# Output products of two mixers started earlier, with their high parts made by ScalarE

## The reference

```python
h = x
for i in range(2):
    u = rmsnorm(h, ln_mix[i])
    if i == 0:      # hs: 4 heads of 256 features; out = sigmoid(o) * rmsnorm(hs)
        mix = mlstm_mixer(u, mlstm_w_in, mlstm_b_gate, mlstm_norm, mlstm_w_out)
    else:           # o: 8 heads of 128 features; (rmsnorm(o) * (1 - lam_init)) @ w_out
        mix = diff_attention_mixer(u, diff_w_in, diff_lam, diff_norm, diff_w_out, i)
    h = h + mix
    h = h + square(relu(rmsnorm(h, ln_mlp[i]) @ w_up[i])) @ w_down[i]
return rmsnorm(h, ln_f)
```

## Time and profile before

| what | us |
|---|---|
| median of 3 runs | 2381.99 |
| lowest and highest of them | 2379.33, 2382.75 |
| the profiled execution: its own time | 2383.44 |
| its span in the trace | 2381.7 |
| TensorE busy in it (share of the span) | 2279.4 (96%) |
| VectorE, ScalarE, GpSimd busy | 1594.4, 888.8, 882.0 |

### The profile page before, as it was taken

One profiled execution on the slowest core, in us unless ns is written; L12 is line 12 of the kernel. 1 busy time (PEld: TensorE's weight loads), 2 busy tenths in 40 slices (PEclk: granted clock), 3 DMA queues, 4 the chain that ended last, 5 costly groups with the idle time before them and its releaser, 6 DMA issues.

```text
span 2381.7 us, 28693 instructions
## 1 busy us (share of the span) xinstructions
PE 2279.4 (96%) x10601; PEld 1880.6 (79%) x10601; DVE 1594.4 (67%) x1988; ACT 888.8 (37%) x1471; POOL 882.0 (37%) x672
## 2 busy tenths in 40 slices
PE   6999998899999999999899999987999999999998
PEld 5788886687888888888688888865878888888887
DVE  7534343569948749579467677775579849578396
ACT  3131122135434334344144444453145334343345
POOL 5433327410213233232476666656500233233230
PEclk9999999999999999999899999997999999999999
DMA  6111111246162442630522322212255352532601
GB/s 180 45 33 39 35 35 53 71 155 263 59 257 106 158 178 71 229 107 1 159 62 55 80 61 62 62 46 87 94 189 195 138 198 71 216 137 103 251 1 71
DMA packets 128834, 262.62 MB, mean 110 GB/s; under 512 B 7217, under 2 KB 81122, under 8 KB 121314
## 3 DMA queue, kind: packets, MB, share of 16 engines
q1 hardware_dynamic: 128290, 260.13, 32.2%
q10 hardware_dynamic: 448, 1.18, 0.1%
HBM read 202.56 MB, written 41.94 MB: 103 GB/s over the span
## 4 chain that ended last, share of the span: by engine, by line
PE 82%; DVE 8%; POOL 5%; ACT 2%; issue 2%; DMA 1%; SPq 0%; ACTq 0%; POOLq 0%; DVEq 0%
PE aps L913 10%; PE aps L915 9%; PE aps L917 9%; PE dps L813 6%; PE dps L815 6%; PE dps L814 5%; PE mps L913 3%; PE dps L913 3%; PE mps L915 3%; PE dps L915 3%; PE mps L917 3%; PE dps L917 3%; PE dps L795 3%; PE dps L796 3%; PE dps L797 3%; PE mps L1133 2%
## 5 line engine op out<-in xcount | busy, mean ns | idle before, releaser
L659 POOL TENSOR_TENSOR w_hi<-w_raw,ones 128x256 fp32r<-128x256 f32 (+1 forms) x127 | 175.7, 1404 | 486.9 <-PE dps L815 266.7
L813 PE MATMUL dps<-one_hi,w_hi 128*128 128x512 f32 x608 | 256.2, 421 | 1.2 <-POOL w_lo L664 1.2
L913 PE MATMUL aps<-b_ring,w_hi 128*128 128x512 f32 x640 | 249.9, 390 | 2.0 <-issue 2.0
L917 PE MATMUL aps<-b_ring,w_hi 128*128 128x512 f32 x640 | 249.0, 389 | 0.0
L915 PE MATMUL aps<-b_ring,w_lo 128*128 128x512 f32 x640 | 249.0, 389 | 0.0
L815 PE MATMUL dps<-one_lo,w_hi 128*128 128x512 f32 x608 | 238.5, 392 | 0.0
L814 PE MATMUL dps<-one_hi,w_lo 128*128 128x512 f32 x608 | 237.8, 391 | 0.0
L1708 DVE TENSOR_TENSOR b_ring<-h,b_ring 128x1024 fp32r<-128x1024 f32 x120 | 206.5, 1728 | 5.6 <-ACT b_ring L1322 5.6
L751 POOL TENSOR_TENSOR s_blk<-s_blk,a 128x1024 f32<-128x1024 f32 x24 | 68.6, 2860 | 377.6 <-DVE w_lo L1690 251.8
L664 POOL TENSOR_TENSOR w_lo<-w_raw,w_hi 128x256 fp32r<-128x256 f32 (+1 forms) x127 | 172.0, 1375 | 5.0
L795 PE MATMUL dps<-one_hi,w_hi 128*128 128x512 f32 x384 | 153.5, 400 | 11.8 <-POOL w_lo L664 4.9
(11 more groups left out here) (298 smaller groups left out, 5593.6 us busy)
## 6 DMA issues: line engine op xcount, KB each, us to landing
b_ring<-xs SPq DMA_DIRECT2D x42, 2048.0 KB, 7.9
xs<-b_ring SPq DMA_DIRECT2D x14, 2048.0 KB, 7.4
a<-in_w_up SPq DMA_DIRECT2D x16, 1024.0 KB, 5.4
a<-in_w_down SPq DMA_DIRECT2D x16, 1024.0 KB, 7.5
w_raw<-in_mlstm_w_in SPq DMA_DIRECT2D x24, 512.0 KB, 3.9
w_raw<-in_diff_w_in SPq DMA_DIRECT2D x24, 512.0 KB, 4.1
hspill<-h SPq DMA_DIRECT2D x2, 4096.0 KB, 12.8
h<-hspill SPq DMA_DIRECT2D x16, 512.0 KB, 3.4
```

The lines of the kernel that those rows point to most:

```text
L659: last = nc.gpsimd.tensor_tensor(w_hi[:, slot, cut], w_raw[:, slot, cut], ones[:, :].unsqueeze(1).broadcast_to([P, piece, P]), ALU.mult)
L813: nc.tensor.matmul(dps[:, half], w_hi[:, slot, k], rh, start=(k == 0), stop=False)
L913: nc.tensor.matmul(to[:, n], wh, ring[:, 0, k], start=new and k == 0, stop=False, skip_group_check=not new)
L917: last = nc.tensor.matmul(to[:, n], wh, ring[:, 1, k], start=False, stop=(k == 3), skip_group_check=not new)
```

## The change

The panels n = 0 and n = 1 of the output product both get their early tiles during the last head, and the work for that moves between engines:

1. Table `FILL` replaces `EARLY_AT`. It names for each place (step, part) the pairs (n, k) of panel and tile whose six products stand there. New places are (0, 1), ahead of the wait for `nm_ready` in layer 0, and (9, 0) and (9, 1), ahead of and behind the last transposes.
2. The early tiles' high parts are made by ScalarE (`high_early`, one instruction a tile): in layer 0 all six behind the sigmoid and ahead of the first step, in layer 1 behind the steps that `HIGH_AT` names. GpSimd makes only the low parts. ScalarE also makes the high parts of the weights of panels 1 and 2 (`high_out`), GpSimd their low parts (`split_out`). Panel 2 has its split weights in `a0_hi` and `a0_lo`, so that they needn't wait for a slot.
3. Panel 0's sum over the early tiles is added to `h` during the last head by VectorE (`add_partial`, in step 3 of layer 0 and step 6 of layer 1), which frees `dps` for panel 1. Its late tiles are summed in `mps` after the head and added by `add_rest`. Panel 1's late tiles follow in `dps`.
4. SyncE loads the weights of panels 2 and 3 ahead of the read-backs of `h`. The loop over the last panels is written out.

```diff
-    EARLY_AT = [[3, 4, 5, 6, 7, 8], [3, 4, 5, 6, 7, 8, 8]]
+    FILL = [{(0, 1): [(0, 0), (0, 1)], (1, 0): [(0, 2)], (1, 1): [(0, 3)], (2, 0): [(0, 4)], (2, 1): [(0, 5)],
...
+    PARTIAL_AT = [3, 6]
+
+    HIGH_AT = {2: [0, 1], 3: [2, 3], 4: [4, 5], 5: [6]}
...
         @block.gpsimd
...
-            def split_early(layer):
+            def split_early(layer, start, end):
 
                 hi, lo = one
-                pool.wait_ge(half_done, 2 * G_OUT[layer])
...
+                for t in range(start, end):
                     pool.wait_ge(y_early_hi, EARLY[0] * layer + t + 1)
...
+                            last = nc.gpsimd.tensor_tensor(
+                                lo[t // 4][:, half, t % 4, cut], h[:, t, half * HALF + c:half * HALF + c + PIECE * P],
+                                hi[t // 4][:, half, t % 4, cut].bitcast(f32), ALU.subtract)
                     last.then_inc(y_early, 1)
...
                 split(g, 1, (g + 1) // 2)
-                split_early(layer)
-                split(g + 1, 0, (g + 1) // 2)
-                pairs(g + 2, g + 8)
...
+                split_early(layer, 0, 4)
+                split_out(layer, 1)
+                split_early(layer, 4, EARLY[layer])
+                if layer == 0:
+                    pool.wait_ge(hy_ready, 2 * MH)
+                else:
+                    pool.wait_ge(on_ready, AH)
+                split_out(layer, 2)
+                for n in range(3, NT):
+                    split(g + n, (g + n) % 2, (g + n + 1) // 2)
...
         @block.tensor
...
+            def early_tile(layer, s, part):
+
+                g = G_OUT[layer]
+                for n, k in FILL[layer].get((s, part), []):
+                    last_k = EARLY[layer] - 1 if n == 0 else NT - 1
+                    if k == 0:
+                        pe.wait_ge(w_split, g + n)
                     pe.wait_ge(y_early, EARLY[0] * layer + k + 1)
-                    out_tile(layer, half, k)
+                    for half in range(2):
+                        if k == 0:
+                            pe.wait_ge(evac, 2 * (g + n) + half - 1)
+                        last = out_tile(layer, n, half, k, dps[:, half], 0, last_k)
...
+                for n in range(2):
+                    for half in range(2):
+                        for k in range(first, NT):
+
+                            pe.wait_ge(hid_ready, HID_OUT[layer] + LATE[layer] * half + k - first + 1)
+                            if n == 0:
+                                last = out_tile(layer, 0, half, k, mps[:, half], first, NT - 1)
+                            else:
+                                last = out_tile(layer, 1, half, k, dps[:, half], 0, NT - 1)
+                        last.then_inc(rest_done if n == 0 else half_done, 1)
+                for n in range(2, NT):
+                    for half in range(2):
+                        half_panel(g + n, (g + n) % 2, half, *one, weights=weights_of(layer, n))
...
         @block.scalar
...
             def mlstm_core(hd, last=False):
...
                 nc.scalar.activation(mo[:, :, :], mo[:, :, :], ACT.Sigmoid).then_inc(sig_ready, 1)
+                if last:
+                    for t in range(4):
+                        high_early(0, t)
+                    high_out(0, 1)
+                    for t in range(4, EARLY[0]):
+                        high_early(0, t)
...
                     step(hd, s, more)
+                    if not more:
+                        for t in HIGH_AT.get(s, []):
+                            high_early(1, t)
...
+            def add_partial(layer):
+
+                dve.wait_ge(first_reloaded, 16 * (layer + 1))
+                for half in range(2):
+                    add_h(G_OUT[layer], 0, half)
+
+            def add_rest(layer, half):
+
+                cut = slice(half * HALF, (half + 1) * HALF)
+                dve.wait_ge(rest_done, 2 * layer + half + 1)
+                nc.vector.tensor_tensor(h[:, 0, cut], h[:, 0, cut], mps[:, half], ALU.add).then_inc(rest_out, 1)
```

More of the change, by code:

```diff
@@ L519, in mixer_loads @@
                     repeat_q(AH - 1)
+                for p in range(2, 4):
+                    g = G_OUT[layer] + p
+                    load_panel(g, g % 2, tiles(w, p * P))
                 for t in range(NT):
@@ L525, in mixer_loads @@
                         sp.wait_ge(hid_ready, HID_OUT[layer] + LATE[layer] + t - EARLY[layer] + 1)
-                    sp.dma_start(h[:, t], hspill[:, t]).then_inc(reloaded[t >= EARLY[layer]], 16)
-                with sp.Fori(1, 4) as i:
+                    back = first_reloaded if t == 0 else reloaded[t >= EARLY[layer]]
+                    sp.dma_start(h[:, t], hspill[:, t]).then_inc(back, 16)
+                with sp.Fori(2, 4) as i:
                     for p in range(2):
@@ new lines, in split_out @@
+            def split_out(layer, n):
+                hi, lo = weights_of(layer, n)
+                slot = (G_OUT[layer] + n) % 2
+                elsewhere[0] += 1
+                pool.wait_ge(out_hi, 2 * layer + n)
+                for t in range(0, NT, PIECE):
+                    cut = slice(t, t + PIECE)
+                    last = nc.gpsimd.tensor_tensor(lo[:, cut], w_raw[:, slot, cut], hi[:, cut].bitcast(f32),
+                                                   ALU.subtract)
+                last.then_inc(w_split, 1)
@@ L784, in _, with half_panel @@
         def _(pe):
-            def half_panel(g, slot, half, hi, lo, ready=None, base=0, hook=None):
+            def half_panel(g, slot, half, hi, lo, ready=None, base=0, weights=None, hook=None):
                 if half == 0:
@@ L935, in mlp, with out_tile @@
                             broadcast_rstd(e, mps)
-            def out_tile(layer, half, k):
-                g, slot, (hi, lo) = G_OUT[layer], G_OUT[layer] % 2, one
+            def out_tile(layer, n, half, k, to, first, last):
+                (wh, wl), (hi, lo) = weights_of(layer, n), one
                 rh, rl = piece(hi, k, half), piece(lo, k, half)
-                nc.tensor.matmul(dps[:, half], w_hi[:, slot, k], rh, start=(k == 0), stop=False)
-                nc.tensor.matmul(dps[:, half], w_lo[:, slot, k], rh, start=False, stop=False)
-                return nc.tensor.matmul(dps[:, half], w_hi[:, slot, k], rl, start=False, stop=(k == NT - 1))
@@ L945, in early_tile @@
-            def early_tile(layer, s, half):
-                for k in range(EARLY[layer]):
-                    if EARLY_AT[layer][k] != s:
-                        continue
-                    if k == half == 0:
-                        pe.wait_ge(w_split, G_OUT[layer])
-                        pe.wait_ge(evac, 2 * G_OUT[layer])
-                    pe.wait_ge(y_early, EARLY[0] * layer + k + 1)
-                    out_tile(layer, half, k)
-            def out_product(layer):
-                g = G_OUT[layer]
-                for half in range(2):
-                    for k in range(EARLY[layer], NT):
-                        pe.wait_ge(hid_ready, HID_OUT[layer] + LATE[layer] * half + k - EARLY[layer] + 1)
-                        last = out_tile(layer, half, k)
-                    last.then_inc(half_done, 1)
-                panels(g, g % 2, 2, *one, skip=1)
-                with pe.Fori(1, 4) as i:
-                    panels(g + 2 * i, g % 2, 2, *one)
+                nc.tensor.matmul(to, wh[:, k], rh, start=(k == first), stop=False)
@@ L1025, in mlstm_core @@
                 feed(4)
+                early(0, 1)
                 pe.wait_ge(nm_ready, hd + 1)
@@ L1287, in a_split @@
                     act.wait_ge(half_done, 2 * (G_OUT[layer] + 6 + a))
+                else:
+                    act.wait_ge(half_done, 2 * (G_OUT[layer] + 3))
                 nc.scalar.activation(kt_view(A_HI[a % 3]), half_of(RAW[name], q), ACT.Copy).then_inc(a_hi, 1)
@@ L1673, in out_product @@
                     late = d >= EARLY[layer]
-                    dve.wait_ge(reloaded[late], 16 * sum((LATE if late else EARLY)[:layer + 1]))
+                    if d > 0:
+                        dve.wait_ge(reloaded[late],
+                                    16 * sum((LATE if late else [n - 1 for n in EARLY])[:layer + 1]))
                     for half in range(2):
-                        add_h(G_OUT[layer] + d, d, half)
+                        if d == 0:
+                            add_rest(layer, half)
+                        else:
+                            add_h(G_OUT[layer] + d, d, half)
                         emit(2 * layer + 1, d, half, 16 * (2 * layer + 1) + 2 * d + half)
```

93 lines of the change are left out of this document (61 added, 32 removed), and 5 rows, old and new, of the table FILL.

## The result

The changed kernel takes 2392.3 us (median of 5, 2391.8 to 2395.6), the kernel before 2381.8 (2378.3 to 2382.8) measured beside it. The ratio is 1.0053, 95% interval 1.0042 to 1.0064: about 10.5 us slower, a difference that stands clear of the measurement. Measured again later it gave 2392.0, ratio 1.0035 (1.0022 to 1.0048). The forecast was 2385.5. The profiled execution took 2395.61 us, span 2393.8.

A forecast was written before the change was run, and what follows sets the result against it. TensorE holds 82% of the chain of waits, GpSimd the stretch the change touches. Layer 0's -0.1 and layer 1's +3.5 give +3.4 us, 2386.8 on the profiled execution; less 1.45, 2385.4, forecast as 2385.5, range 2376 to 2394.

The forecast's parts named there:

- T0: Time of TensorE's first late product in a layer's output product; before the change 433.76 us in layer 0, 1659.97 in layer 1.
- the clock: TensorE at half clock after its idle time behind T0: 1.4 us lost in layer 0, 2.3 in layer 1.
- Products moved: Extra products done ahead of T0: 36 in layer 0 (-8.2 us), 42 in layer 1 (-9.5 us).
- T0 in layer 0: Layer 0's last head: GpSimd's low parts start behind VectorE's copy, T0 comes 4.5 us later, bounds 2.9 and 6.0.
- Behind T0 in layer 0: Third panel waits for VectorE's third add, bank free 9.1 us behind T0: 2.2 us lost, plus 1.4 of clock.
- T0 in layer 1: Layer 1's last head: early tiles wait for their high and low parts, T0 comes 6.8 us later, bounds 4.0 and 9.0.
- The rounds: Layer 1's early tiles: products, values, ScalarE's copies, high part, low part in turn; 8.4 to 9.0 us each, taken as 9.3.
- Behind T0 in layer 1: Third panel's bank free 9.3 us behind T0, low part slowed beside GpSimd: 3.9 us lost, plus 2.3 of clock.
- Other edits: Weight loads, read-back of tile 0 (9 us of cover), ScalarE's instructions, written-out loop: no cost, up to 1 us each if wrong.
- A: Rival: layer 1's rounds at half clock (T0 +9.0), 2.8 us clock loss per layer; 2389.5 us; chance 0.41.
- B: Rival: VectorE's third add in time for panel 2, together -6.4 us, 2375.6; chance 0.16 shared with the full-gain rival.
- The wait for L1735: Sign: TensorE waits before panel 2's first product, 2 to 4 us in layer 0, 5 to 7 in layer 1.

The follow-up runs named there:

- run 11: On run 5, ScalarE makes layer 1's high parts sooner, as in run 6: 2383.8 us, ratio 1.0003.
- run 6: On run 1, ScalarE makes the high parts of layer 1's early tiles sooner (three, two, two behind steps 2 to 4): 2367.0 us, ratio 0.9934.
- run 4: On the changed kernel, 24 products that nobody reads fill TensorE's wait ahead of the third panel: 2388.3 us, ratio 1.0022.
- run 5: On the changed kernel, the second panel's early tiles are not moved but computed behind the first panel's late products: 2391.8 us, ratio 1.0040.
- run 7: On run 1, GpSimd makes the low parts of all early tiles before those of the second panel's weights: 2382.5 us, ratio 0.9998.
- run 1: On the changed kernel, VectorE does tile 0's rest adds and the second panel's first two adds before squares and low parts: 2374.1 us, ratio 0.9960.
- run 8: On run 6, GpSimd's order of run 7, with SyncE's read-back of tile 0 ahead of the third and fourth panels' loads: 2365.5 us, ratio 0.9922.
- run 3: On the changed kernel, GpSimd splits the fourth panel's weights only after VectorE's add of the second panel's first half: 2385.7 us, ratio 1.0010.

## Why the prediction was wrong

The time lies inside the range, at its upper end, and the sum had the right sign. But I called it no measurable change, and it is one. That the range held it is partly luck: the bounds as stated for T0, the waits and the clock add up to -6.2 and +9.0, not to -3.5 and +11, and +10.3 lies outside them (what I had allowed for the other edits did not come). By its own steps:

- **Products moved**, -8.2 and -9.5: right, as far as run 11 against run 6 shows it (20.8 us behind T0, with the clock).
- **T0 in layer 0**, +4.5: it was +3.4, about right. A starts 1.04 us later in this trace. Counted from there, ScalarE's first high part was ready when I had said, but GpSimd's first four tiles ended 1.0 us sooner than my 385.3 + 11.2 gave. GpSimd did not start behind VectorE's copy but inside it, at 384.75, when 0.77 us of the copy were left; the first of its sixteen pieces took 1.35 us where the next took 0.73, and ended 0.58 behind the copy. So the copy cost 0.6 us and not the 1.6 that I took, which is about what T0 came sooner. In the changed kernel:

```profile
383.29 2.23 DVE L2165 COPY m_cur<-m_next 128x4096 f32<-128x4096 f32 x1
384.75 11.75 POOL L716 TENSOR_TENSOR one_lo<-h,one_hi 128x256 fp32r<-128x256 f32 x16 [9.56 <-ACT one_hi L1532]
```

  The Trainium skill, SBUF — State Buffer, section "SBUF: two separate sides", says that the second of the two fully blocks until the first is done; the trace agrees.
- **Behind T0 in layer 0**, +2.2 of wait and +1.4 of clock: this step failed, and it alone makes 4.4 of the 6.9 us by which the sum was off. I let GpSimd's split meet VectorE in layer 1 only, and took 9.1 us from the rows of before, where no split fell there. In both layers the split starts when TensorE ends the second panel, and that now comes before VectorE's accumulator add and low part. The bank was free at T0 + 12.3, 3.2 later. Half clock lasted 5.8 us, where I took the 2.7 of the earlier trace rows; by run 4 the clock cost 2.6 here and not 1.4 (in layer 1 it cost 1.2, where I took 2.3). With T0 1.1 sooner, -0.1 becomes -0.1 - 1.1 + 3.2 + 1.2 = +3.2; measured +3.4.
- **T0 in layer 1**, +6.8: mis-sized by 2.0. From the place of the first tile on, T0 came 8.8 us later (the other 1.9 of C lie ahead of it, where the code is the same). The rounds were right in sum: from the first tile to the seventh I had 27.9 us, and it took 28.3 (1619.20 to 1647.49), as a long first round of 10.4 and two of 9. What failed is the next step. I had TensorE at full clock from the seventh tile to the second place of step 6, 4.2 us; it took 5.8 (1647.49 to 1653.33), because behind the third wait it ran at half clock, as the products of 0.70 and the transposes of 1.26 show (the same six took 0.82 in the kernel before):

```profile
1647.49 0.70 PE L974 MATMUL dps<-one_hi,w_hi 128*128 128x512 f32 x1 [1.83 <-POOL one_lo L716]
...
1650.13 1.26 PE L1171 MATMUL mps<-ident,ee 128*128 128x128 f32 x6
1651.97 1.60 PE L1177 MATMUL mps<-relu,at 128*128 128x128 f32 x12 [0.58 <-ACT at L1628]
1653.33 0.48 PE L974 MATMUL dps<-one_hi,w_hi 128*128 128x512 f32 x1
```

  I had also charged the six tiles of steps 6 to 8 in full; run 5 gives back only 2.3 us without them. I had that time filled from one side only: the tiles add 8.2 us and take away waits for VectorE and half clock.
- **Behind T0 in layer 1**, +3.9 of wait and +2.3 of clock, D -3.3: it was -3.8. The low part took 2.82 us beside GpSimd, as foreseen, and the bank was free at T0 + 9.8. I had written 9.3; my own terms, 7.8 and the 2.1 that the low part takes longer, give 9.9. The clock, 1.2, made up for it.
- **Other edits**: the read-back of tile 0 was hidden, as I said. Run 7 shows how thin the cover was. I had put it at 9 us, from the load's time at 399 alone. The read-back takes 5 us of that to land, and in run 7 the weights came 5.5 us later while VectorE was ready for the add sooner.

Of the rivals, A came nearest in time and size: its clock term of 2.8 held in layer 0 (2.6) and its T0 term of +9.0 in layer 1 (8.8). Its mechanism held in part: of the three rounds only the first, 10.4 us, ran mainly at half clock. B, the third add in time, became true only when the order was changed. Run 1 then gave 18 us, where the terms that B lets fall away add up to 9.8 (2.2 + 1.4 and 3.9 + 2.3); its time of 2375.6 was near run 1's 2374.1, since the changed kernel had lost more than I forecast.

Of the signs, the waits for low parts at the first tile and at tiles 2, 4 and 6 of layer 1 came as listed. The wait for L1735 was 6.7 us in layer 1, inside my 5 to 7, and 6.5 in layer 0, where I had 2 to 4.

What stays open: how long the half clock lasts behind a wait of a given length. Behind waits of 6.5, 6.7, 3.0 and 4.5 us it lasted 5.8, 2.7, 3.6 and 6.1 us. And the 1.9 us in layer 1 ahead of the first tile. No run separates the half clock in layer 1's first round from the waits.

## What to carry to other kernels

When work is moved ahead of a point, write out for each consumer behind that point what its queue still holds, in order: the freed time is lost if the next bank waits for a row of bookkeeping, and putting the two adds in front was worth 18 us here. Where a chain goes round three engines once per tile, give the first of them several tiles of lead. In SyncE's queue here a load that waited for a semaphore delayed the read-backs behind it (runs 7 and 8), so the cover of a transfer has to be counted from the last thing that the queue ahead of it waits for.

## What the runs showed of the hardware

- Behind T0, VectorE's instructions with two inputs in SBUF stand still beside GpSimd's split and end about 0.55 us behind it (2.14 and 2.82 us instead of 0.69 and 0.75). An add with one input in PSUM does not: 0.68 us beside the low part (run 3). The Trainium skill, SBUF — State Buffer, section "SBUF: two separate sides", states both; I had not applied it to which of VectorE's instructions the split would meet.
- A step without work for TensorE was not free for the steps that followed: in run 5 the same sixteen value products took 3.56 us at half clock, and 2.05 in the changed kernel, with tiles between them.
